# Four waits moved in a streaming-encoder kernel, and the sample's value rows weighted and summed by the matrix engine

## What is computed

```python
mod = silu(c) @ w_ada + b_ada          # shift, scale, gate, twice
lat = rms_norm(ckv, kv_norm_g)         # the latents
x = x + gate1 * (merged @ w_out)
# feed-forward, h2 = modulate(x, ...)
expert, gate = top_k of the keys' scores, softmax     # 128 per token
a = einsum('td,thkd->thk', h2, u_tab[expert])
w = gate * gelu(a)
x = x + gate2 * einsum('thk,thkd->td', w, v_tab[expert])
y = rms_norm(x) * final_g
```

## Time and profile before

| | us |
|---|---|
| median of three executions | 4278.77 (4278.7 to 4281.38) |
| the profiled execution | 4321.2 |
| its span, first to last instruction | 4319.4 |
| PE busy | 3502.0 |
| DVE busy | 2839.2 |
| POOL busy | 1461.3 |
| ACT busy | 388.0 |

### The profile page before, as it was taken

How to read it: one execution, slowest core, us unless ns; L and a number is a source line. 1 busy time by engine, 2 the same in 40 slices (tenths; PEclk the granted TensorE clock), 3 DMA queues, 4 the chain that set the end, 5 groups by cost and what they waited for, 6 DMA issues and landing times.

```text
span 4319.4 us, 39399 instructions
## 1 busy us (share of the span) xinstructions
PE 3502.0 (81%) x14249; PEld 2505.6 (58%) x14249; DVE 2839.2 (66%) x3456; ACT 388.0 (9%) x958; POOL 1461.3 (34%) x1094
## 2 busy tenths in 40 slices
PE   7899999999989999999986989997599998970000
PEld 5465678887845546467765667775476766750000
DVE  5354432237777886776677868986875566557998
ACT  0311110000212111010000011001000000000000
POOL 0000000000024544553343413233533666656764
PEclk9999999999999999989998999999799999995555
DMA  8577555557368998999999957789899999988997
GB/s 331 193 278 275 208 197 191 194 219 287 136 242 332 389 392 351 391 366 392 419 408 416 400 221 308 294 341 420 350 407 379 384 410 409 382 316 353 396 383 320
DMA packets 251314, 1412.71 MB, mean 327 GB/s; under 512 B 35312, under 2 KB 83456, under 8 KB 86144
## 3 DMA queue, kind: packets, MB, share of 16 engines
q0 software_dynamic: 124704, 841.18, 48.3%
q1 hardware_dynamic: 68832, 501.25, 30.0%
q10 hardware_dynamic: 57632, 68.41, 4.5%
HBM read 1359.60 MB, written 51.16 MB: 327 GB/s over the span
## 4 chain that ended last, share of the span: by engine, by line
PE 53%; DVE 17%; DMA 13%; issue 5%; POOL 2%; another core or an unknown queue 2%; PEld 2%; DVEq 2%; ACT 1%; ACTq 1%; PEldq 1%; SPq 0%
PE pq L401 52%; DMA first<-peer_v,experts 8%; DVE pq L1693 7%; DMA first<-peer_u,experts 4%; DVE late L1693 3%; POOL first L1849 2%; PEld pq L401 2%; DMA ring<-wstream 1%; DVE first L1683 1%; PE pq L405 1%; ACT arena L798 1%; DVE arena L1466 1%; DVE arena L1473 1%; DVE arena L1467 1%
## 5 line engine op out<-in xcount | busy, mean ns | idle before, releaser
L401 PE MATMUL pq<-h_last,ring 128*128 128x288 f32 (+2 forms) x6688 | 1712.3, 415 | 169.1 <-issue 78.1
L401 PEld LDWEIGHTS pq<-h_last,ring 128*128 128x128 f32 (+2 forms) x6688 | 1262.0, 191 | 612.3 <-issue 164.0
L1849 POOL DMA_INDIRECT first<-peer_u,experts x256 | 433.3, 1693 | 1731.8 <-DVEq L1528 1243.5
L1849 POOL DMA_INDIRECT first<-peer_v,experts x464 | 628.1, 1354 | 906.7 <-DVEq L1694 789.5
L1693 DVE SCALAR_TENSOR_TENSOR late<-first,wts,late 128x2048 f32<-128x2048 f32 x254 | 597.3, 2352 | 184.8 <-DMA first<-peer_v,experts 172.1
L401 PE MATMUL pq<-first,ring 128*128 128x256 f32 (+2 forms) x3104 | 702.1, 385 | 20.0 <-issue 9.0
L1683 DVE CUSTOM_DVE_ANT_0 first<-first,late 128x2048 f32<-128x2048 f32 x256 | 582.1, 2292 | 192.1 <-DMA first<-peer_u,experts 184.3
L401 PEld LDWEIGHTS pq<-first,ring 128*128 128x128 f32 (+2 forms) x3104 | 572.9, 187 | 143.1 <-issue 43.8
L1693 DVE SCALAR_TENSOR_TENSOR pq<-first,wts,pq 128x2048 f32<-128x2048 f32 x142 | 334.5, 2356 | 103.1 <-DMA first<-peer_v,experts 86.5
L1867 POOL DMA_INDIRECT got<-dots_dram,at_dot x288 | 317.0, 1101 | 126.7 <-issue 93.1
L401 PE MATMUL pq<-arena,ring 128*128 128x256 f32 (+2 forms) x1216 | 303.4, 407 | 46.0 <-DVEq L1435 32.1
(11 more groups left out here) (197 smaller groups left out, 2002.2 us busy)
## 6 DMA issues: line engine op xcount, KB each, us to landing
ring<-wstream SPq DMA_DIRECT2D x478, 1024.0 KB
dots_dram<-wts ACTq DMA_DIRECT2D x8, 2304.0 KB, 8.4
dots_dram<-stage ACTq DMA_DIRECT2D x128, 144.0 KB
first<-peer_v,experts POOLq DMA_INDIRECT x464
got<-dots_dram,at_dot POOLq DMA_INDIRECT x288
first<-peer_u,experts POOLq DMA_INDIRECT x256
out<-arena ACTq DMA_DIRECT2D x6, 512.0 KB, 8.2
o_last<-x_t ACTq DMA_DIRECT2D x5, 576.0 KB, 11.1
```

The lines of the kernel that those rows point to most:

```text
L401: return nc.tensor.matmul(out, lhsT, rhs, start=start, stop=stop)
L1849: g.indirect_dma_start(out=slots[slot], out_offset=None, in_=peer_u if kind == "u" else peer_v, in_offset=bass.IndirectOffsetOnAxis(ap=exp ...
```

## The change

Five edits. (1) ACT computes Silu(cT) right after its first two loads, and the Silu of the rows after the first two pieces of x. (2) In `mixers`, `fill(14)` before the latents is now `fill(9)`, and `fill(8)` behind them `fill(13)`. (3) `take(3)` and `take(6)` are new, on both sides of the memset in front of the second routing; the numbers of N_GATES, N_VAR0, N_SCALE0 and N_LAST are 6, 6, 10 and 2 higher. (4) ACT's `finish` for tile 0 is split: the squares stay at trip 9, the root comes at trip 13. (5) The sample's rows are no longer added by DVE. DVE only forms the eight weights of a batch, ACT multiplies the matrix `cn["stack"]` with each of them (128 x 32, into `stack_w`), and PE multiplies each gathered row with its matrix, four matmuls of 512 columns, into the same PSUM banks throughout; it frees the buffer of the row. The sample's four batches alternate with four of tile 3.

```diff
@@ -214,7 +214,7 @@
         g2b = late[:, 2 * D:3 * D]
         fgb = sb("fgb", [P, D])
         sq_junk = arena[:, 2 * D:3 * D]
-        acc_s = arena[:, D:2 * D]
+        stack_w = arena[:, D:D + TS * SLOTS * TS // P].rearrange("p (c t) -> p c t", t=TS)
         acc_early = arena[:, 3 * D:4 * D]
         ranked = arena[:, 5 * D:5 * D + DN * SLOTS]
         hot_e = arena[:, D:2 * D].rearrange("p (h r k) -> p h r k", h=PH, r=TOPK)
@@ -364,15 +364,16 @@
         NU = len(UNIT)
         TRIPS = NK // 4
         S_COL = QT * SLOTS
-        T_GATES, T_FIN0, T_RANKED, T_STORE0, T_LAST = 7, 9, 14, 15, 16
+        T_GATES, T_FIN0, T_ROOT0, T_RANKED, T_STORE0, T_LAST = 7, 9, 13, 14, 15, 16
         BATCHES = ([(r, t) for r in range(R_ALT) for t in (2, 3)] + [(r, 2) for r in range(R_ALT, TOPK)]
-                   + [(r, QT) for r in range(QS // FB)] + [(r, 3) for r in range(R_ALT, TOPK)])
+                   + [b for r in range(QS // FB) for b in ((r, QT), (R_ALT + r, 3))]
+                   + [(r, 3) for r in range(R_ALT + QS // FB, TOPK)])
         ORDER = ([("u", 0, c) for c in range(SLOTS)] + [("u", 1, c) for c in range(SLOTS)]
                  + [("v", 0, c) for c in range(SLOTS)] + [("x", 0, 0)]
                  + [("v", 1, c) for c in range(SLOTS)] + [("x", 1, 0)]
                  + [("v", t, FB * r + e) for r, t in BATCHES for e in range(FB)])
         TAIL = len(ORDER) - FB * len(BATCHES)
-        N_GATES, N_VAR0, N_SCALE0, N_LAST, N_NEED = 432, 452, 470, 500, TAIL - 1
+        N_GATES, N_VAR0, N_SCALE0, N_LAST, N_NEED = 438, 458, 480, 502, TAIL - 1
         SORT_STEPS = 26
         uses = [0] * (GR + RING)
         N_WIDE = TAIL + 2 * FB * R_ALT
@@ -786,10 +787,20 @@
             tokens_of(og[1], 2 * P, TS, 0)
             pe.wait_ge(tok_ok, 8)
             gate2_rows(1)
-            pe.wait_ge(acc_in, 1)
-            for c in range(4):
-                last = mm(pb[4 + c][0:TS, :], cn["stack"][:, 0:TS], acc_s[:, c * 512:(c + 1) * 512])
-            last.then_inc(sum_ps, 1)
+            pe.wait_ge(y_pre, 3)
+            for i, (r, t) in enumerate(BATCHES):
+                if t != QT:
+                    continue
+                pe.wait_ge(stack_ok, r + 1)
+                for e in range(FB):
+                    slot, use = ENTRY[TAIL + FB * i + e][3:5]
+                    c, row = FB * r + e, slots[slot]
+                    pe.wait_ge(g_in[slot], 16 * (use + 1))
+                    for q in range(4):
+                        last = mm(pb[4 + q][0:TS, :], stack_w[:, c, :], row[:, q * 512:(q + 1) * 512], c == 0, c == QS - 1)
+                    if c == QS - 1:
+                        last.then_inc(sum_ps, 1)
+                    pe.drain().then_inc(g_used[slot], 1)
 
 
         @block.scalar
@@ -799,15 +810,17 @@
 
             act.dma_start(cT[:, :, :], c_t).then_inc(c_in, 16)
             act.dma_start(late[:, 0:2 * D], c_rows.to_broadcast([P, 2 * D])).then_inc(crow_in, 16)
+            act.wait_ge(c_in, 16)
+            a(cT[:, :, :], cT[:, :, :], ACT.Silu).then_inc(silu_ok, 1)
             act.dma_start(bad[:, :], b_ada).then_inc(bada_in, 16)
             act.dma_start(cst[:, :], consts).then_inc(cst_in, 16)
-            for i in range(4):
+            for g in range(2):
+                act.dma_start(og[g][:, 0:4, :], x_t[:, 0:4, CG[g]:CG[g + 1]]).then_inc(x_in[0], 16)
+            act.wait_ge(crow_in, 16)
+            a(late[:, 0:2 * D], late[:, 0:2 * D], ACT.Silu).then_inc(crow_ok, 1)
+            for i in range(1, 4):
                 for g in range(2):
                     act.dma_start(og[g][:, 4 * i:4 * i + 4, :], x_t[:, 4 * i:4 * i + 4, CG[g]:CG[g + 1]]).then_inc(x_in[i], 16)
-            act.wait_ge(c_in, 16)
-            a(cT[:, :, :], cT[:, :, :], ACT.Silu).then_inc(silu_ok, 1)
-            act.wait_ge(crow_in, 16)
-            a(late[:, 0:2 * D], late[:, 0:2 * D], ACT.Silu).then_inc(crow_ok, 1)
 
             def root(n, c0, c1):
 
@@ -1162,13 +1175,20 @@
             act.wait_ge(zero_out, 16 * NH)
             gelu(1, SLOTS, SLOTS)
             dense_out(0, True)
-            def finish(n, t, y):
+            def finish_squares(n, t, y):
                 m = rows(t)
                 act.wait_ge(y_pre, n + 1)
                 a(sq_junk[0:m, :], y[0:m, :], ACT.Square, accum_out=stat[0:m, 0, t:t + 1])
                 act.drain().then_inc(y_ss, 1)
+
+            def finish_root(n, t):
+                m = rows(t)
                 act.wait_ge(y_rs, n + 1)
                 a(stat[0:m, 1, t:t + 1], stat[0:m, 1, t:t + 1], ACT.Sqrt).then_inc(y_rs2, 1)
+
+            def finish(n, t, y):
+                finish_squares(n, t, y)
+                finish_root(n, t)
 
             def store(n, t, y):
                 act.wait_ge(y_ok, n + 1)
@@ -1184,8 +1204,11 @@
                 dense_out(i)
             act.wait_ge(rt_used, 2 * PH)
             act.wait_ge(route_ok, 2)
-            finish(0, 0, h2_acc[0])
-            with act.Fori(T_FIN0, T_STORE0) as i:
+            finish_squares(0, 0, h2_acc[0])
+            with act.Fori(T_FIN0, T_ROOT0) as i:
+                dense_out(i)
+            finish_root(0, 0)
+            with act.Fori(T_ROOT0, T_STORE0) as i:
                 dense_out(i)
             store(0, 0, h2_acc[0])
             with act.Fori(T_STORE0, TRIPS) as i:
@@ -1197,12 +1220,17 @@
             to_sbuf(g2b_s, bank=0)
             finish(1, 1, h2_acc[1])
             store(1, 1, h2_acc[1])
+            def weighted_stacks(r):
+                act.wait_ge(wts_s_ok, r + 1)
+                for c in range(FB * r, FB * r + FB):
+                    last = a(stack_w[:, c, :], cn["stack"][:, 0:TS], ACT.Identity, scale=wts[:, S_COL + c:S_COL + c + 1])
+                last.then_inc(stack_ok, 1)
+
+            weighted_stacks(0)
             finish(2, 2, x2_tok[2])
             store(2, 2, x2_tok[2])
-            act.wait_ge(acc_ok, 1)
-            for c in range(4):
-                a(acc_s[:, c * 512:(c + 1) * 512], pb[4 + c][:, :])
-            act.drain().then_inc(acc_in, 1)
+            for r in range(1, QS // FB):
+                weighted_stacks(r)
             finish(3, QT, x2_tok[QT])
             store(3, QT, x2_tok[QT])
             finish(4, 3, x2_tok[3])
@@ -1396,11 +1424,11 @@
                 dve.drain().then_inc(prob_ok, 1)
 
             def mixers(g, fill):
-                fill(14)
+                fill(9)
                 latents(g, fill)
                 if g == 0:
                     dve.wait_ge(crow_ok, 1)
-                fill(8)
+                fill(13)
                 for i in range(NH):
                     if g == 0:
                         for q in range(2):
@@ -1768,9 +1796,11 @@
                 add_out(1, j)
                 take(2)
             second_norm(1)
+            take(3)
             dve.wait_ge(proj, unit_done((1, "wq", 0)))
             v.memset(routing[1].s_head[:, :, 2, :, :], 0.0)
             dve.drain().then_inc(s_clear, 1)
+            take(6)
             route(1, take)
             take(4)
             ranking = sort_by_expert()
@@ -1785,7 +1815,7 @@
                 dve.wait_ge(ss_in[lap], 16 * FB * (i // LAPS + 1))
                 r, t = BATCHES[i]
                 c = t * SLOTS + FB * r
-                acc = quads[1][:, :] if t == QT else acc_early if t == 3 and r < R_ALT else acc_of[t]
+                acc = acc_early if t == 3 and r < R_ALT else acc_of.get(t)
                 if t == 3 and r == R_ALT:
                     for j in range(2):
                         dve.wait_ge(a_free[j], NK // 2 + 1)
@@ -1793,6 +1823,9 @@
                     v.tensor_copy(acc, acc_early)
                 v.tensor_tensor(wts[:, c:c + FB], got[:, lap, :], gates[:, c:c + FB], ALU.mult)
                 dve.drain().then_inc(ss_free[lap], 1)
+                if t == QT:
+                    dve.drain().then_inc(wts_s_ok, 1)
+                    return
                 for e in range(FB):
                     add_row(TAIL + FB * i + e, acc)
                     for step in steps.get(e, ()):
@@ -1814,17 +1847,14 @@
                 v.tensor_tensor(y, y, tmp, ALU.add)
                 dve.drain().then_inc(y_pre, 1)
 
-            def sample_added():
-                dve.drain().then_inc(acc_ok, 1)
-
             i2 = 2 * R_ALT
             i3 = i2 + TOPK - R_ALT
-            i4 = i3 + QS // FB
+            i4 = i3 + 2 * (QS // FB)
             steps = {i3 - 4: {0: [lambda: finish_var(1, 1)], 4: [lambda: finish_scale(1, 1, h2_acc[1])]},
                      i3 - 1: {FB - 1: [lambda: last_sum(2)]},
-                     i3: {3: [lambda: finish_var(2, 2)], 7: [lambda: finish_scale(2, 2, x2_tok[2])]},
-                     i4 - 1: {FB - 1: [sample_added]}, i4: {7: [sample_sum]},
-                     i4 + 1: {3: [lambda: finish_var(3, QT)], 7: [lambda: finish_scale(3, QT, x2_tok[QT])]}}
+                     i3 + 1: {3: [lambda: finish_var(2, 2)], 7: [lambda: finish_scale(2, 2, x2_tok[2])]},
+                     i4: {3: [sample_sum]},
```

(1 more changed line is left out.)

2 lines of the change are left out of this document (1 added, 1 removed).

## The result

The changed kernel took 4248.86 us (median of four executions, 4242.36 to 4266.46), the kernel before 4279.88 beside it. The ratio is 0.9936, with an interval of 95% from 0.991 to 0.9962; by the ratio that is 27 us, by the medians 31. So the change is worth 27 to 36 us. Executions of one kernel lie up to 24 us apart here, which is why the traces are compared in groups further down.

What follows compares the result with a forecast made beforehand. PE was taken to set the pace up to the dense loop, then weights and value rows sharing full DMA, then rows alone. -11 -13.5 -39 +10 = -53.5 from 4278.77 gave 4225 us; forecast 4212 to 4240, range 4192 to 4258.

Steps and rivals of the forecast that it cites:

- Silu first: Start: PE begins at 6 to 8 us, first `ada_cols` moves from 45.47 to about 34; -11 us (-6 to -16).
- Latents: Second group: nine dots first let PE's transposes start near 1284.3 instead of 1298.87; -13.5 us (-8 to -15).
- both gains reach the dense loop whole: Between front and dense loop: PE's chain was taken to carry the -11 and -13.5 us through undiminished.
- Gap rows: Before the second routing: nine rows in DVE's idle time, 2.6 us each off the DMA-full stretch; -23 us (0 to -35).
- Tile 0's end: Dense loop: 63 us PE wait goes, about 17 us sort wait comes; -39 us with the nine rows (-25 to -60).
- the first profile's slack of 24 us: Before row 646: DVE's 24.00 us wait, 18.2 of it taken as absent from ordinary runs.
- the first profile's excess: Whole program: 42.4 us over the median, split into 24.2 behind ACT's copy and 18.2 of DVE's wait before row 646.
- Tail: Sample rows: PE sums them, a pair of batches takes 43.3 us against 40.2; +10 us (-10 to +20).
- The row of the old stack sum: Tail: eight matmuls took 5.08 us from half clock, 1.55 more; taken to show the clock returns inside the burst.
- the rival with PE at 1.2 GHz throughout: Tail: PE stays at half clock, a pair takes 70 us, the whole 4331 us; chance 0.04.
- The front's gains not carrying: Rival, front to dense loop: row blocks, rotate and sort hold PE; -26 us in all, 4253 us; chance 0.13.
- The stall on the path: Rival, dense loop: rows have slack, PE's end decides; -57 us there, -71.5 in all, 4207 us; chance 0.22.

Runs made afterwards that it cites:

- silu_only: Kernel before with only the earlier Silu of cT and its reordered Silu of the rows: 4287.13 us, ratio 0.9992.
- fill_later: Kernel before with all edits but the tail's, the five dots moved behind the eighth head's work: 4238.34 us, ratio 0.9873.
- front_later: Kernel before with the earlier Silu and nine dots ahead of the latents, the other five behind the eighth head: 4281.05 us, ratio 0.9978.
- gap_only: Kernel before with only the nine value rows around the memset before the second routing, step numbers moved: 4277.7 us, ratio 0.9973.
- before: The kernel before, unchanged, in its first profile: that execution took 4321.2 us, against a median of 4278.77.
- before_again: The kernel before, unchanged, timed and profiled once more: 4290.94 us, ratio 1.0005.
- tail_only: Kernel before with only the sample's rows weighted and summed on PE, alternating with tile 3: 4292.34 us, ratio 1.0012.
- ranked_nt: Kernel before with all edits but the tail's, and the ranked transposes one trip later: 4247.52 us, ratio 0.9901.
- gap_tile0: Kernel before with only the nine value rows around the memset and the split finish of tile 0: 4247.42 us, ratio 0.9895.
- front_only: Kernel before with only the earlier Silu and nine dots ahead of the latents: 4276.8 us, ratio 0.998.

## Why the prediction was half right

- **Silu first (forecast -11).** -3 to -5 (0.9992, and 5.0 us at `ada_cols`). The step that failed is ACT ready for its copies at "30 to 33", with the queueing of x "unchanged": the issues end at 39.5, since ACT first waits 7.13 us for the load of the rows, for which the sum had only the 3.60 us of the Silu. The wait behind PE's early start was named in the right place and sized too small.
- **Latents (forecast -13.5).** At the transposes of the latents the mean of six old traces is 1302.6, `silu_only` is at 1296.4, and the mean of the seven with both edits at 1282.4: -14 for edit 2, as forecast. Then the step "both gains reach the dense loop whole, since the stages between are PE's chain" failed, and it carries the miss. With edits 1 and 2 as they are, seven executions have the memset at 2544.1 on average; six executions whose code up to there is the old one have it at 2550.7 (2545.2 to 2553.8). That is 7 us of 24.5. The timed runs agree: 0.998 and 0.9964. In the heads 6 us go to rotates that stand on DVE behind dots waiting for gathers (3.41 us of wait and 7.5 of loss in the changed kernel's trace, with a granted clock of 0.77 behind it). In the FoX heads another 4 go, where traces of the same code differ by PE's clock, and 3 in the merges, where DVE sets the pace: the kernel before has PE waiting 30.00 us for it at 2375.65, a row that the prediction did not read. Open is why PE's clock falls where it does, and whether the place of the five dots matters; `fill_later` and `front_later` contradict each other. Edit 2 was not run alone.
- **Gap rows (forecast -23).** They fit their gaps as worked out. By `needed_blocks`, behind row 513, they had saved 24 to 29 us: without its wait of 11.07 `gap_only` is there 730.8 us after the memset, and `before`, `before_again` and `tail_only` are at 754.5 to 759.9. But alone they brought only 9 us of that to row 646.
- **Tile 0's end.** The wait went, the one for the sort came (25 us, forecast 17), rows and not PE's end decided (`ranked_nt`), and the first profile's slack of 24 us wasn't there in other executions. With the gap rows -39 was forecast, -36 is what the traces show on average, and -45 (38 to 52) what `gap_tile0` was timed at. The total was right, its parts were not: the sum adds -23 and -16, and alone they are worth 9 and 11. What wasn't seen is that the two edits need each other. Also wrong is how the first profile's excess was laid out. Taking off 18.2 us puts row 646 near 3847 and PE's end within 6 us of the rows; in `before_again` the row comes at 3868 and PE ends 30 us ahead, in `tail_only` at 3850 and 18 us. The 24.2 us behind ACT's copy did belong to the first profile alone (454.6 us from row 646 to the end there, 429.6 in the second).
- **Tail (forecast +10).** +8 to +9: pairs of 42.5 to 45.0 us for 43.3. The row of the old stack sum was the right one to go by, and the rival with PE at 1.2 GHz throughout is out: PE gets its clock back inside each batch, and eight rows took 31.7 us (4120.93 to 4152.6) where 31.9 was worked out.
- **The sum.** By the traces it is -7 in front, -36 in the dense loop and +9 in the tail, -34 in all, against 27 to 36 us in the timed runs. Of the 20 us that are missing from the forecast the front has 18.
- **The rivals.** The front's gains not carrying had 0.13 and a sum of -26 (4253). It is the one whose mechanism came, and its conditions were met: PE's row blocks waited for weights and for ACT's copies, a rotate waited behind dots, and the sort held PE for 25 us. Its size is only partly right: it gave the front -13 and the dense loop -25, and they are -7 and -36. The stall on the path fell with `ranked_nt` and `before_again`.

The best kernel seen has edits 1 to 4 alone: 0.9878 and 0.9896, and 0.9873 with the five dots later, so 45 to 55 us faster than before by the timed runs.

## What to carry to other kernels

A gain early in a program reaches the end only if nothing between is paced by something else: before you carry it through a stage, look for waits of the leading engine on one that does filler work, and ask whether that filler waits for DMA. Two edits that each remove one of two alternating limits are worth little apart and much together, so price them in pairs. And before a wait in one profile is taken as slack, profile the same kernel again; here the same code stood 15 us apart after 2500 us.

## What the runs showed of the hardware

In one stretch of code PE has its full clock of 2.4 GHz in one execution and falls to 1.2 GHz for a part of it in another, in the middle of its work. 36 matmuls of 256 columns, with pauses of 0.26 and 0.17 us ahead of them, took 7.95 or 10.12 us in executions of the same code (`tail_only` and `gap_tile0`). The granted clock in the stretch was 0.98 in `tail_only` (1879 to 1887) and 0.73 in `front_only`, which took 10.12 us as well. The Trainium skill (TensorE: Matmul & The Clock Gate, HAM oscillation) tells of such swings for work with pauses for data; here a pause of 3.41 us stood ahead of the fall at 1474.77, none over 0.26 us ahead of the other.
